# A decoder layer on one core: the first expert's turned rows by a one-hot product of the token rows on chip

## The reference

```
s = sigmoid(xt @ router_w)
sel = (s + router_b).reshape(-1, N_GROUPS, EXPERTS_PER_GROUP)
...                         # best group by the sum of its top two, then top two inside it
combine = einsum('nk,nke->ne', w, one_hot(e_idx, N_EXPERTS))
for e in range(N_EXPERTS):
    h = silu(xt @ e_wg[e]) * (xt @ e_wu[e])
    y = y + combine[:, e:e + 1] * (h @ e_wd[e])
```

## Time and profile before

| what | us |
|---|---|
| three runs, median (lowest, highest) | 1470.54 (1467.07, 1470.69) |
| the profiled execution, its own time | 1473.95 |
| the profiled execution, its span | 1471.7 |
| PE busy | 1338.8 (91% of the span) |
| PEld busy | 1170.1 (80%) |
| DVE busy | 788.7 (54%) |
| ACT busy | 535.5 (36%) |
| POOL busy | 403.3 (27%) |

### The profile page before, as it was taken

How to read it: one execution, slowest core, us unless ns; L and a number is a source line. 1 busy time by engine, 2 the same in 40 slices (tenths; PEclk the granted TensorE clock), 3 DMA queues, 4 the chain that set the end, 5 groups by cost and what they waited for, 6 DMA issues and landing times.

```text
span 1471.7 us, 20300 instructions
## 1 busy us (share of the span) xinstructions
PE 1338.8 (91%) x8065; PEld 1170.1 (80%) x8065; DVE 788.7 (54%) x1068; ACT 535.5 (36%) x734; POOL 403.3 (27%) x306
## 2 busy tenths in 40 slices
PE   4997998989999888999999999887994999999985
PEld 4987998989888777989998877765883788888862
DVE  7137275572726577722321430322446799999936
ACT  1243421526221454111001011343103688788840
POOL 8464555545245233223332000011000000011010
PEclk9998999999999999999999999997995999999998
DMA  7553323322133212234336301246523899999933
GB/s 242 162 187 102 108 85 111 108 82 86 45 94 87 63 46 65 65 93 119 103 108 201 122 29 57 87 181 241 213 86 95 322 406 410 410 411 412 408 141 128
DMA packets 153498, 239.95 MB, mean 163 GB/s; under 512 B 6400, under 2 KB 111033, under 8 KB 145089
## 3 DMA queue, kind: packets, MB, share of 16 engines
q1 hardware_dynamic: 131472, 177.98, 34.6%
q0 software_dynamic: 14544, 51.52, 9.9%
q10 hardware_dynamic: 7393, 9.20, 1.9%
HBM read 214.08 MB, written 24.60 MB: 162 GB/s over the span
## 4 chain that ended last, share of the span: by engine, by line
PE 49%; DMA 3%; DVE 3%; issue 1%; ACT 1%; POOL 0%; DVEq 0%; POOLq 0%; SPq 0%; ACTq 0%
PE bank L1110 46%; DMA kv_k<-in_cache_mem_k_dram 2%; PE bank L1552 1%; PE bank L1437 1%; PE bank L1135 1%; DVE x_tok L2271 0%; PE bank L1560 0%; DMA yb<-expert_rows,ints 0%; DVE small L2261 0%; ACT kv_t L773 0%; DMA kv_v<-in_cache_mem_v_dram 0%; DMA xg<-x_scratch,table 0%; ACT pT L773 0%; DMA expert_rows<-y_out 0%; DVE expert_weights_lo L2045 0%
## 5 line engine op out<-in xcount | busy, mean ns | idle before, releaser
L2045 DVE TENSOR_TENSOR expert_weights_lo<-expert_weights,expert_weights_hi 128x2048 fp32r<-128x2048 f32 x96 | 218.5, 2290 | 34.5 <-ACT expert_weights_hi L1034 33.2
L1034 ACT ACTIVATE expert_weights_hi<-expert_weights 128x2048 fp32r<-128x2048 f32 x96 | 182.7, 1916 | 22.1 <-PE bank L1110 14.6
L1110 PE MATMUL bank<-x_hi,gate_weights_hi 128*128 128x288 f32 x512 | 163.8, 320 | 12.1 <-ACT gate L932 11.4
L1110 PE MATMUL bank<-x_hi,gate_weights_lo 128*128 128x288 f32 x512 | 152.2, 297 | 0.0
L1110 PE MATMUL bank<-x_lo,gate_weights_hi 128*128 128x288 f32 x512 | 152.1, 297 | 0.0
L1110 PE MATMUL bank<-x_hi,mixer_weights_hi 128*128 128x288 f32 x448 | 137.9, 308 | 0.9 <-ACT q_all L813 0.9
L1110 PE MATMUL bank<-ob,branch_weights 128*128 128x288 f32 (+1 forms) x512 | 134.5, 405 | 0.0
L1110 PE MATMUL bank<-x_lo,mixer_weights_hi 128*128 128x288 f32 x448 | 134.5, 300 | 0.0
L1110 PE MATMUL bank<-x_hi,mixer_weights_lo 128*128 128x288 f32 x448 | 134.3, 300 | 0.0
L2326 POOL TENSOR_TENSOR mixer_weights_lo<-mixer_weights,mixer_weights_hi 128x1024 fp32r<-128x1024 f32 x52 | 128.2, 2466 | 4.2
L932 ACT ACTIVATE gate<-bank,pc 128x288 f32<-128x288 f32 x64 | 31.7, 501 | 226.4 <-PE bank L1110 223.8
(11 more groups left out here) (418 smaller groups left out, 2914.9 us busy)
## 6 DMA issues: line engine op xcount, KB each, us to landing
expert_weights<-in_e_wg_dram SPq DMA_DIRECT2D x32, 1024.0 KB, 8.8
expert_weights<-in_e_wu_dram SPq DMA_DIRECT2D x32, 1024.0 KB, 9.1
expert_weights<-in_e_wd_dram SPq DMA_DIRECT2D x32, 1024.0 KB, 8.9
mixer_weights<-in_w_in_dram SPq DMA_DIRECT2D x36, 512.0 KB, 4.0
gate_weights<-in_w_in_dram SPq DMA_DIRECT2D x32, 512.0 KB, 4.1
branch_weights<-in_w_branch_dram SPq DMA_DIRECT2D x32, 256.0 KB, 3.7
kv_k<-in_cache_mem_k_dram POOLq DMA_DIRECT2D x8, 1024.0 KB, 7.5
kv_v<-in_cache_mem_v_dram POOLq DMA_DIRECT2D x8, 1024.0 KB, 5.5
```

Of the source, the lines that this page charges most:

```text
L1034: act.activation(w_hi[n % HIS][:], w_raw[n % RAW][:], ACT.Copy).then_inc(w_hi_done, 1)
L1110: return pe.matmul(out, lhsT, rhs, start=start, stop=stop)
L2045: dve.tensor_tensor(w_lo[n % RAW][:], w_raw[n % RAW][:], w_hi[n % HIS][:].bitcast(F32), ALU.subtract).then_inc(w_lo_done, 1)
```

## The change

For the first expert alone, the turned rows are no longer made by table, gather and transpose. DVE makes a one-hot `first_hot` (five tiles of 128 tokens by 128 places) straight from the "pos" counts. PE multiplies the token rows on chip by it: for each of the eight column groups, five matmuls over the token tiles, with a 128x128 piece of `x_tok` standing and 128 columns of `first_hot` moving, both plain f32 (the other products of an expert are fp32r). The result lands in the same banks "eX" and "eX'", and ACT and DVE split it as before. The table is still made, for the other experts; POOL now starts with the gathers of experts 1 and 2. On DVE `weights_lo(2)` moves from ahead of the counting to behind the copy of the table, and `xgT_lo` of the first expert moves ahead of that copy.

More of the change, by code:

```diff
@@ L613, in trunk @@
             sem("slots_written"), sem("tile_experts"))
+        first_ready = sem("first_expert_one_hots")
         hot_ready, xg_idx, xg_landed = sem("slot_table_one_hots"), sem("gather_index"), [sem("rows0_gathered"), sem("rows1_gathered")]
@@ L2228, in _ @@
                 elif what == "x":
[L2229 to L2233, removed]
+                    if n:
+                        rows_lo(n)
                 else:
```

## The result

The changed kernel takes 1480.18 us (median of 5 runs, 1476.28 to 1482.82), against 1469.58 for the kernel before (5 runs, 1467.07 to 1470.69): a ratio of 1.0067, interval 1.0051 to 1.0084. It is slower by 10.6 us; 1469.2 had been forecast. The profiled execution took 1482.82 us, with a span of 1480.7.

The account below looks back on a forecast made before the run. The prediction took DVE's queue to bound the start of expert 1's gate, with which the rest moves; -1.5 us there plus 0.2 for the clock gave -1.3, so 1470.54 became 1469.2 us, range 1465.8 to 1472.8.

Parts of the forecast that it names:

- The product: PE's one-hot product for the first expert: 40 plain f32 matmuls, 80 records, 11.4 us, ending at 1127.1.
- 63 behind it at 0.114: In PE's product, 63 records after the 4.0 us low-clock phase, at 0.114 us each as in the attention product.
- rival 2: PE's clock stays low through the product: 17.6 to 19.9 us, kernel 1476.4 to 1478.7 us; chance 0.06.
- the second start: PE's start of expert 1's gate, with which the rest moves as a block; forecast 1148.3 against 1149.82.
- Rival 3: Stride of eight in x_tok slows full-clock passes: product about 15 us, kernel 1472.6; chance 0.05 shared with the edge.
- the edge: The change does nothing in time: product ends near 1128.6, kernel 1470.5 us; chance 0.05 shared with Rival 3.
- four in 0.45 us: PE's transposes at 1145.68, cited against Rival 3: same stride in xg, none slow at full clock.
- DVE up to the second start: DVE's queued work sets the second start, 21.2 us after the product's end, 1.5 us earlier than before.
- -1.3 was the sum: Whole kernel: -1.5 us from the second start plus 0.2 for PE's clock there.
- Rival 1: PE's chain, not DVE's, sets the second start: whole earlier start comes through, gain 5.7, 1464.8 us; chance 0.10.
- Its other estimate of the product at full clock: From the Trainium skill: PE's 40 matmuls as 160 times 0.081, 13.0 us, kernel about 1473.
- The distance behind the second start: From the second start to the kernel's end, claimed to stay as before, 321.9 us.

Follow-up runs that it names:

- 2: The changed kernel with the last token tile padded by zeros from 64 to 128 rows; ratio to before 1.0042, product 19.34 us.
- 5: The changed kernel with 128 rows and standing pieces of neighbouring columns, expert 0's gate and up weights loaded to match; ratio to before 0.9987.
- 11: The kernel of 9 with extra unread matmuls, 12 ahead of the counts and four behind; ratio to before 0.9930, median 1460.50 us.
- experiment 6: The kernel of 5 without its padding, so the last token tile has 64 rows again; ratio to before 1.0025, product 15.05 us.
- 1: The changed kernel with 20 extra unread matmuls, 16 ahead of the counts and four behind; ratio to before 1.0067.
- 4: The changed kernel with DVE's weights_lo(2) ahead of the first expert's xgT_lo and nineteen small instructions behind expert 1's; ratio to before 1.0058.
- 9: The kernel of 5 with the DVE order of 4; ratio to before 0.9946.
- 3: The changed kernel with token rows moving in place of the one-hots; one execution, 1481.13 us, product 23.89 us.

## Why the prediction was wrong

**The step that failed** is *The product*: "63 behind it at 0.114". 11.4 us had been forecast, 23.9 came. The price of a record was wrong for these pieces, and the changes of the row count had been put at nothing, without a reason. The difference of 12.5 in parts that the runs separate:

- 7.35 us is the step of eight in the standing piece (2 against 5). At full clock a record takes 0.24 in place of 0.11 (9.17 / 80, in 11).
- 4.56 us is the change between 128 and 64 rows (the change against 2). Taken in the other order, over experiment 6, the step has 8.85 and the rows 3.06.
- 0.6 is the clock's rise, which the forecast had 4.0 us after the product's start. In 5 the window 1118 to 1120 still has 0.56, so it came nearly 6 us after the start at 1113.87. In the change itself it did not come at all.

The row that the price came from, the attention product, has neither: its pieces lie straight and have 128 rows.

The clock did stay low, as in rival 2, and the second start of 1162.89 (1161.9 without the later choice) lies even beyond that rival's 1158. But its cause is refuted: with the full clock given for the product's first 3.2 us (1), it took 23.66, and 13 us at full clock in 2 did not change the pace of the records. Low clock and slow product stand side by side in the profile, and reading the one as the cause of the other would have been the wrong lesson. The 0.30 a record was also above rival 2's own bound of 0.25, which no clock explains.

**Rival 3** had the main cause at half its size: a product of 15 us, 3.6 over the forecast, in place of 7.35, with a chance of 0.05 that it shared with the edge. It was set aside because the transposes read `xg` with the same step and are fast. They are, but they are not free of it. Their weight loads, and below them those of the transposes of the hidden rows `hs`, which lie straight, both in the kernel before:

```profile
L1552 PEld LDWEIGHTS bank<-cst,xg x128: 185/193/230, 1129.3 to 1394.0; 128*128 128x128 f32 x128
L1560 PEld LDWEIGHTS bank<-cst,hs x64: 138/139/143, 1156.7 to 1416.7; 128*128 128x128 f32 x64
```

The step makes a transpose's load longer too, 193 ns in place of 139. It does not show in the time: in the chain eight transposes of `xg` take 0.89 us and four of `hs` 0.44, 0.11 a record in both. The "four in 0.45 us" of the prediction told the pace of the records and not the length of their loads. In the product the step adds 144 ns to a load (336 in place of 192), and there the pace of the records goes with it. It is also not the same case, as a transpose is one record and this product's plain f32 multiplication is two. Why the step costs more in the product stays open.

The Trainium skill, "Advanced Engine Details and Errata", section "SBUF Cachelines", has 16-byte lines of which each should be hit twice at least to hide the latency of the access. The prediction did not weigh it. The product agrees on where the edge lies: a step of 8 bytes still hits each line twice and was nearly free (0.118 us a record against 0.112), and steps of 16 and 32 bytes were not (18.91 and 19.34 us). The transposes, with 32 bytes, have longer loads too, but lose no time. That the lines are the mechanism is not shown by any run.

**The steps that held.** The one-hots were ready at 1116.70, 2.95 after the choice (forecast 2.9), with `first_hot` at 0.82 (forecast 0.83). *DVE up to the second start* said E + 21.2 for the time from the product's end. In 5, where the rest ran as supposed, it was 1125.86 to 1146.85 = 20.99, PE idled 6.91 (forecast 7), and DVE idled 3.78 ahead of the second `xgT_lo` (forecast 4). In the change it was 22.2, as the table's ten matmuls ran at the low clock (2.62) and DVE waited 1.15 for them; rival 2 had priced this at 1.2. That DVE's queue set the second start is shown by 4 and 9. With the forecast of everything else, the sum is thus -1.5 + 12.5 + 1.0 + 0.1 = 12.1.

With both causes mended the change comes near to what had been forecast: 5 has 0.9987, or 1.9 us off 1470 (interval 0.6 to 3.2), and -1.3 was the sum; by the distance from the choice it is 0.97. **Rival 1** came true only once DVE's queue was cleared as well (9). The prediction said that it would need `weights_lo` at 1.4 us; by its own terms it is 1.6 (six pieces would have to save 4.1 us, 0.7 each). Its other estimate of the product at full clock, 13.0 us, does not hold: in 11 it took 9.17, as by the row of the attention product (9.3).

**The distance behind the second start** was given as 321.9 and came to 317.8, because the profiled execution of before took longer at its end. The forecast was made from that execution's own time and did not rest on it.

## What to carry to other kernels

The price of a matmul taken from another row holds for the same kind of load: look at the step, the rows and the type of the standing piece before using it. Here, at full clock, straight or every second f32 column was twice as fast as every fourth or eighth, and a tile filled up with zeros was faster than one of half the rows. A low clock beside a slow stretch is not yet its cause; the pace of the same records at full clock tells. And here an earlier producer paid in full only when work was moved out of the queue behind it (DVE's), in part into the time in which that engine idles anyway: 4.9 us from the choice in 9, against 1.0 in 5.

## What the hardware showed that was not expected

- Weight loads of the plain f32 product with a step of four or eight take 329 to 336 ns at the median also at full clock, with a step of one or two 192 to 196. Its records then come every 0.23 to 0.24 us in place of 0.11 to 0.12.
- A change between 128 and 64 rows leaves a gap in the loads each way, 0.22 us at the low clock (the change) and 0.12 at full clock (6).
- The load of a transpose with a step of eight takes 193 ns in place of 139, with the records at the same pace.
- In experiment 1 the clock fell from 1.00 to 0.50 within a stretch in which PE was busy for all of each window; with straight loads and full rows it stayed at 1.00 (11). With the step and the 64-row tile together (the change, 3, 4) it never rose inside the product; with one of the two alone (2, 6) it did, a little over 6 us in. PE was busy in all of these windows.
